# Dense projections cut by contraction steps over the slots of four mixers

## The reference

```python
for layer in range(DEPTH):                                   # DEPTH = 2
    need_ctx = layer < DEPTH - 1
    mod_l = adaln_params(c, w_mod[layer], b_mod[layer])      # silu(c) @ w_mod + b_mod, 6 parts of 1024
    mod_c = adaln_params(c_ctx, w_mod[layer], b_mod[layer])
    p_l = split_cols(modulate(x, norm1_g[layer], mod_l[0], mod_l[1]) @ w_in[layer])
    p_c = split_cols(modulate(ctx, norm1_g[layer], mod_c[0], mod_c[1]) @ w_in[layer])
    a_l, a_c = diff_attention(...)            # DA: softmax minus lambda times a second softmax
    b_l, b_c = hgrn2_mixer(...)               # HG: gated recurrence in both directions
    n_l, n_c = neighbourhood_attention(...)   # NA: 8 x 16 window on the 8 x 64 grid, and the context
    w_l, w_c = window_gqa(...)                # SW: band of 128 tokens, and the context
    x = x + mod_l[2] * (concat([a_l, b_l, n_l, w_l]) @ w_out[layer])
    x = x + mod_l[5] * (square(relu(modulate(x, norm2_g[layer], mod_l[3], mod_l[4]) @ w_ff1[layer])) @ w_ff2[layer])
    # with need_ctx the same for ctx with mod_c
```

## Time and profile before

| | us |
|---|---|
| median of 3 runs (2523.86 to 2529.58) | 2527.3 |
| profiled execution | 2523.21 |
| its span | 2521.4 |
| TensorE busy (82% of the span) | 2078.6 |
| VectorE busy (46%) | 1159.5 |
| ScalarE busy (30%) | 766.8 |
| GpSimd busy (24%) | 610.0 |
| mean granted clock | 0.908 |

### The profile page before, as it was taken

One profiled execution on the slowest core, in us unless ns is written; L12 is line 12 of the kernel. 1 busy time (PEld: TensorE's weight loads), 2 busy tenths in 40 slices (PEclk: granted clock), 3 DMA queues, 4 the chain that ended last, 5 costly groups with the idle time before them and its releaser, 6 DMA issues.

```text
span 2521.4 us, 29860 instructions
## 1 busy us (share of the span) xinstructions
PE 2078.6 (82%) x12484; PEld 1705.4 (68%) x12484; DVE 1159.5 (46%) x1782; ACT 766.8 (30%) x1225; POOL 610.0 (24%) x263
## 2 busy tenths in 40 slices
PE   5779786687775698999999997879688639899998
PEld 3667564466664586888888885658477536688887
DVE  2544536555499715222221316454685884522322
ACT  2522222223333325222221315232344432522321
POOL 0121010001166122222222221301001552344432
PEclk9889797778898798999999998989799778999999
DMA  7312020323165011122112212111001011232231
GB/s 261 59 51 84 1 67 1 101 88 80 42 204 193 5 51 49 52 67 67 57 62 67 68 50 39 55 33 34 17 18 51 0 34 51 67 100 88 96 100 67
DMA packets 178918, 168.86 MB, mean 67 GB/s; under 512 B 29200, under 2 KB 176096, under 8 KB 178656
## 3 DMA queue, kind: packets, MB, share of 16 engines
q1 hardware_dynamic: 176704, 161.18, 20.9%
q10 hardware_dynamic: 2080, 5.77, 0.8%
HBM read 159.07 MB, written 2.10 MB: 64 GB/s over the span
## 4 chain that ended last, share of the span: by engine, by line
PE 67%; DVE 17%; ACT 9%; issue 4%; POOL 2%; DMA 1%; ACTq 0%; SPq 0%; DVEq 0%; POOLq 0%
PE gp L691 53%; PE sp L823 3%; PE gp L858 2%; ACT DA_p L1184 2%; POOL HGx_kd L613 2%; PE sp L734 1%; PE tp L838 1%; ACT nt L1097 1%; PE sp L814 1%; PE gp L712 1%; DVE small L1578 1%; DVE sp L1453 1%; PE sp L921 1%; DVE sp L1452 1%; DMA raw<-in_w_mod 1%
## 5 line engine op out<-in xcount | busy, mean ns | idle before, releaser
L637 POOL TENSOR_TENSOR wlo<-raw,whi 128x2048 fp32r<-128x2048 f32 x98 | 452.4, 4617 | 1684.3 <-ACT whi L1079 1684.1
L691 PE MATMUL gp<-xhi,whi 128*128 128x512 f32 (+1 forms) x1584 | 584.1, 369 | 114.5 <-DVE xlo L1473 53.0
L691 PE MATMUL gp<-xlo,whi 128*128 128x512 f32 (+1 forms) x1584 | 570.8, 360 | 0.0
L691 PE MATMUL gp<-xhi,wlo 128*128 128x512 f32 (+1 forms) x1584 | 569.3, 359 | 0.0
L691 PEld LDWEIGHTS gp<-xhi,whi 128*128 128x128 f32 x1584 | 312.1, 197 | 170.2 <-issue 55.8
L691 PEld LDWEIGHTS gp<-xlo,whi 128*128 128x128 f32 x1584 | 311.7, 197 | 43.0 <-issue 1.7
L691 PEld LDWEIGHTS gp<-xhi,wlo 128*128 128x128 f32 x1584 | 310.8, 196 | 43.2
L1079 ACT ACTIVATE whi<-raw 128x2048 fp32r<-128x2048 f32 x98 | 186.8, 1908 | 426.3 <-PE gp L691 425.2
L1833 DVE SCALAR_TENSOR_TENSOR xT<-gp,mods,xT 128x512 f32<-128x512 f32 x120 | 78.6, 662 | 475.9 <-PE gp L691 475.9
L691 PE MATMUL gp<-hhi,whi 128*128 128x512 f32 (+1 forms) x768 | 273.7, 356 | 9.3 <-ACT frel L1393 6.3
L691 PE MATMUL gp<-hlo,whi 128*128 128x512 f32 (+1 forms) x768 | 272.1, 354 | 0.0
(11 more groups left out here) (304 smaller groups left out, 2864.3 us busy)
## 6 DMA issues: line engine op xcount, KB each, us to landing
raw<-in_w_ff SPq DMA_DIRECT2D x64, 1024.0 KB, 5.3
raw<-in_w_mod SPq DMA_DIRECT2D x48, 1024.0 KB, 5.3
raw<-in_w_in SPq DMA_DIRECT2D x20, 1024.0 KB, 5.1
raw<-in_w_in SPq DMA_DIRECT2D x24, 256.0 KB, 4.3
raw<-in_w_out SPq DMA_DIRECT2D x8, 768.0 KB, 4.7
bias<-e SPq DMA_DIRECT2D x96, 32.0 KB
xin<-in_x ACTq DMA_DIRECT2D x1, 2048.0 KB, 9.2
raw<-in_w_out SPq DMA_DIRECT2D x16, 128.0 KB, 4.7
```

The costliest lines, as they stand in the source:

```text
L637: nc.gpsimd.tensor_tensor(wlo[:, s % 2, :, :], raw[:, index[splits[s]] % 2, :, :], whi[:, s % 2, :, :].bitcast(F32), ALU.subtract).then_in ...
L691: mm = pe.matmul(out, lhs, rhs, start=(i == 0 and j == 0), stop=(i == KT - 1 and j == 2))
```

## The change

The table of filler is made anew. A dense group may now be cut along its contraction: a slot holds (unit, group, first step, end step), and a group that is begun in one slot goes on in the next in the same bank. Work is weighed and dealt out evenly over the slots of a mixer. All modulations leave NA and SW. Layer 0 has 14 in DA and 10 in HG (before: 4, 2, 12 and 22), layer 1 has 7 in DA and 9 in HG (before: none). Rows and turns of one modulation stand in neighbouring slots. The other engines walk a table ENDS with only the groups that end in a slot.

ScalarE rounds a weight unit as soon as the unit that used the same rounded buffer is done; only where the unit two places before is a modulation must its row have been reached.

VectorE reads all groups that end in a slot, except the last, before `finish`, and the last behind it.

```diff
-    mods = [("mod", 0, j, i) for j in range(2, 6) for i in range(4)] + [("mod", 1, j, i) for j in range(6) for i in range(4)]
+    mods = [("mod", l, j, i) for l, js in ((0, range(2, 6)), (1, range(6))) for j in js for i in range(4)]
+    counts = {("NA", 0): 0, ("SW", 0): 0, ("DA", 0): 14, ("HG", 0): 10, ("NA", 1): 0, ("SW", 1): 0, ("DA", 1): 7, ("HG", 1): 9}
...
+                k0 = 0
+                for k in range(KT):
+                    done += w
+                    if done * n >= (s + 1) * total and k < KT - 1:
+                        slots[s].append((u, c, k0, k + 1))
+                        k0 = k + 1
+                        s = min(s + 1, n - 1)
+                slots[s].append((u, c, k0, KT))
...
 FILL = fill_plan()
+ENDS = {key: [[(u, c) for u, c, _, b in slot if b == KT] for slot in slots] for key, slots in FILL.items()}
...
-            def dense(u, *cs, ready=None):
+            def dense(u, *cs, ready=None, part=range(KT)):
                 s = split_no[u] % 2
-                if cs[0] == chunks_of(u)[0]:
+                if cs[0] == chunks_of(u)[0] and part[0] == 0:
                     pe.wait_ge(lo_done, split_no[u] + 1)
                 for c in cs:
-                    start_group(N(u, c))
+                    if part[0] == 0:
+                        start_group(N(u, c))
...
             def after_unit(u):
 
-                reached[0] = max(reached[0], index[u])
+                reached[0] = max(reached[0], last_group(u))
                 while nexts[0] < len(splits):
                     s = nexts[0]
                     v = splits[s]
-                    if index[v] - 2 > reached[0]:
+                    before = units[index[v] - 2]
+                    if before[0] == "mod" and last_group(before) > reached[0]:
                         return
-                    before = units[index[v] - 2] if index[v] >= 2 else None
-                    if before and before[0] == "mod" and last_group(before) > last_group(u):
-                        return
-                    if s >= 2 and last_group(splits[s - 2]) > last_group(u):
+                    if s >= 2 and last_group(splits[s - 2]) > reached[0]:
                         return
...
                 if which == 1:
-                    wait_read(dve, ("mod", 0, 1, 3) if l == 0 else ("mod", DEPTH - 1, 5, 3))
+                    wait_read(dve, ("mod", l, 1, 3))
...
+                    fill(ENDS[m, l][n][:-1])
                     finish(n + 1)
-                    fill(FILL[m, l][n])
+                    fill(ENDS[m, l][n][-1:])
                     output(n)
```

More of the change, by code:

```diff
@@ L139, in fill_plan @@
         tiles = 6 if l < DEPTH - 1 else 4
-        for m, names, n_mods, n_slots in (("NA", ("SWq", "SWkv"), 4, 2 * tiles), ("SW", ("DAq", "DAk", "DAv"), 2, 2 * tiles),
-                                          ("DA", ("HGq", "HGi"), 12, 4 * tiles), ("HG", (), 22, 6 * tiles)):
-            items = [(("prj", l, n), c) for n in names for c in chunks_of(("prj", l, n))]
-            todo = [mods.pop(0) for _ in range(n_mods if l == 0 else 0)]
-            slots = [[] for _ in range(n_slots + 1)]
-            work = [[x] for x in items]
-            for i, u in enumerate(todo):
-                work.insert((i + 1) * (len(items) + i) // (len(todo) + 1) if items else i, [(u, "row"), (u, "turn")])
-            last = -1
-            for i, w in enumerate(work):
-                a = i * n_slots // len(work)
-                if len(w) == 2:
-                    slots[a].append(w[0])
-                    slots[a + 1].insert(0, w[1])
-                else:
-                    slots[a] += w
+        for m, names, n in (("NA", ("SWq", "SWkv"), 2 * tiles), ("SW", ("DAq", "DAk", "DAv"), 2 * tiles),
+                            ("DA", ("HGq", "HGi"), 4 * tiles), ("HG", (), 6 * tiles)):
+            chunks = [(("prj", l, name), c) for name in names for c in chunks_of(("prj", l, name))]
+            units = [mods.pop(0) for _ in range(counts[m, l])]
+            work = []
+            put = 0
+            for i, (u, c) in enumerate(chunks):
+                work.append((u, c, 2 if c[0] != "tok" and c[1] == 0 else 1))
+                closing = i + 1 < len(chunks) and chunks[i + 1][0] != u
+                while not closing and put < len(units) * (i + 1) // len(chunks):
+                    work.append((units[put], "row", 3))
+                    put += 1
+            work += [(u, "row", 3) for u in units[put:]]
+            total = sum(8 * w if c != "row" else 4 for _, c, w in work)
+            slots = [[] for _ in range(n + 1)]
+            s, done, turn = 0, 0, None
+            for u, c, w in work:
+                if c == "row":
+                    if turn:
+                        slots[s].append(turn)
+                    slots[s].append((u, "row", 0, KT))
+                    turn = (u, "turn", 0, KT)
+                    done += 4
+                    s = min(max(s + 1, done * n // total), n)
+                    continue
+                if turn:
+                    slots[s].append(turn)
+                    turn = None
+                k0 = 0
[6 more added lines that the diff above has]
+                slots[s].append((u, c, k0, KT))
+                if 10 * done * n >= (10 * s + 6) * total:
+                    s = min(s + 1, n - 1)
+            if turn:
+                slots[s].append(turn)
@@ L179, in dense_order @@
         for m in ("NA", "SW", "DA"):
-            groups.extend((u, c, one) for slot in FILL[m, l] for u, c in slot)
+            groups.extend((u, c, one) for slot in FILL[m, l] for u, c, a, _ in slot if a == 0)
         for n in ("HGf0", "HGf1", "HGg"):
             whole(("prj", l, n))
-        groups.extend((u, c, both) for slot in FILL["HG", l] for u, c in slot)
+        groups.extend((u, c, both) for slot in FILL["HG", l] for u, c, a, _ in slot if a == 0)
         for j in range(4):
@@ L721, in fill @@
             def fill(slot):
-                for u, c in slot:
+                for u, c, a, b in slot:
                     if u[0] == "mod":
@@ L725, in fill @@
                     else:
-                        dense(u, c)
+                        dense(u, c, part=range(a, b))
             def norm_sums(l, which, ks):
@@ L1283, in hgrn @@
                         if idx >= 4:
-                            fill(FILL["HG", l][idx - 4])
+                            fill(ENDS["HG", l][idx - 4])
                         idx += 1
                 read_out(ntile - 1)
-                for slot in FILL["HG", l][-5:]:
+                for slot in ENDS["HG", l][-5:]:
                     fill(slot)
```

23 lines of the change are left out of this document (12 added, 11 removed).

## The result

The changed kernel takes 2541.0 us (median of 5 runs, 2536.9 to 2543.3) against 2527.3 (also the median of 5 runs now): the ratio is 1.0050, with an interval of 1.0037 to 1.0064. It is slower by half a per cent, 13 us above the forecast of 2528. That is inside the whole range, 2505 to 2549, and outside the 2518 to 2538 that the forecast gave itself.

The account below looks back on a forecast made before the run. The prediction took TensorE's chain as the bound, with VectorE the floor in short DA slots and the bound in HG. Its terms summed to +0.5 us on 2523.2: 2523.7, or 2528 for the median; range 2505 to 2549.

Parts of the forecast that it names:

- HG: HG of both layers: 0.24 us per modulation; twelve fewer in layer 0 give -2.9, nine more in layer 1 +2.2.
- NA of layer 1: NA, layer 1: same work in equal pieces, two waits go and two handovers come; +1.5 us.
- DA of layer 0: DA, layer 0: slots of 147.8 us plus low clock sum to 161.4 against 178.1, -16.7; bounds -30 and +2.
- NA and SW of layer 0: NA and SW, layer 0: modulations, waits and low clock leave; -15.9 and -14.2 us.
- A slot of DA: Slots of DA: TensorE goes on 1.3 us after an early-read turn; 3.9 stays in slots 3, 5, 15, 17.
- DA of layer 1: DA, layer 1: seven modulations come with VectorE as floor; 117.7 against 89.0 us, +28.7; bounds +14 and +36.
- The end of DA: End of DA: late HGf0 and HGf1 loads hold the squares on ScalarE; +10.6 us in layer 0, +6.8 in layer 1.
- a sign of being wrong: Wrong if HG changed by more than 7, DA of layer 1 below 105, or squares within 2 us of last value product.
- rival 3: Low clock after each bank handover costs 1.2 instead of 0.4 in DA's 22 short gaps: +18, 2546 us; chance 0.25.
- Rival 2: The two stalls behind late loads, at the ends of DA, do not decide: -17.4, 2511 us; chance 0.11.
- rival 1: Modulations in DA of layer 1 are cheap, 1.55 us each: -14, DA of layer 0 -8; 2506 us; chance 0.20.
- The lock's price beside the sum: VectorE and GpSimd's shared port lock: remainders under softmax, three in SW, one in DA, some 4 us; sum would be +4.0.

Follow-up runs that it names:

- e7: The kernel before with only ScalarE rounding a weight unit as soon as its rounded buffer is free; 2520.4 us, ratio 0.9969.
- e6: The changed kernel with every read put ahead of the softmax whose bank is wanted again in the same slot; 2527.2 us, ratio 0.9993.
- e1: The changed kernel with all 16 modulations of layer 1 moved into HG of layer 0, which then has 26; 2508.0 us, ratio 0.9928.
- e5: The changed kernel with the modulations of DA put two chunks earlier in both layers; 2514.9 us, ratio 0.9940.
- e4: The changed kernel with the old modulation counts: 4, 2, 12 and 22 in layer 0, none in layer 1; 2507.5 us, ratio 0.9915.
- e12: The changed kernel with HG's rows spread evenly and each turn in the slot behind its row, both layers; 2536.1 us, ratio 1.0027.
- e2: The changed kernel with nine modulations moved from HG of layer 1 to HG of layer 0, which then has 19; 2535.8 us, ratio 1.0040.
- e9: The kernel before with early rounding on ScalarE and the first reads of a slot ahead of the softmax; 2483.4 us, ratio 0.9815.
- e8: The kernel before with only VectorE's reads of all groups of a slot but the last put before the softmax; 2486.5 us, ratio 0.9832.
- e10: e9 with the six modulations of NA and SW of layer 0 moved into HG (28 there), groups whole; 2467.1 us, ratio 0.9755.
- e3: The changed kernel with useless TensorE work in HG of layer 0: rows spread, turns over two slots and issued six times; 2547.1 us, ratio 1.0080.
- e11: Modulation places of e10, split table for DA of layer 0 alone, e6's read order, rows two chunks earlier; 2473.1 us, ratio 0.9788.

## Why the prediction came out as it did

The range held, and the sign of most terms; the forecast itself, no change, was 13 us too low. That it was no more is partly luck: by the traces HG came out 14.7 us above its terms and NA of layer 1 5.8, while DA of layer 0 came out 4.1 below. Taken by its steps:

- **NA and SW of layer 0: right.** -17.3 and -13.4 against -15.9 and -14.2. e7 shows the wait for `wlo` alone to be worth 6 to 8 us. Neither of the two profiled executions had the collision of the last section in NA; with it, the same instructions took 141, and NA's part would have been near -9.
- **A slot of DA: right.** 3.9 behind turns that are a slot's only end, 1.3 behind the others; e6 takes the first away for 13.4 us. From end of scores to end of scores the four slots with the long wait took 12.5, 12.4, 12.2 and 12.2 us, against 10.4 and 2.0 of low clock in the forecast. DA of layer 0 came to 157.3 against 161.4, DA of layer 1 to 116.9 against 117.7. The second total is right for a partly wrong reason: I gave the split one piece's late read and the modulations 3.6 each, and e1 gives the split 12 and each modulation 2.2.
- **The end of DA: right**, +13.7 and +6.4 against +10.6 and +6.8, and e5 shows the loads to be the cause. The squares came 12.8 us behind the value product where I had 11.4.
- **HG: the step that failed.** I priced a modulation at 0.24 us in either layer, from the difference of the two layers per level, took twelve away for -2.9 and added nine for +2.2. Over the same cut as the forecast's, layer 0 went up by 8.6 us and layer 1 by 9.4, both more than the 7 that I had named as a sign of being wrong (6.7 and 7.3 in the levels of the table). In layer 0 the number of modulations has no price that the runs show: 19, 22 and 26 took 105.9, 104.8 and 106.7 in the new placing, and 10 took 104.0 to 108.1. What shows is the place of the turn. With 22 modulations the new placing cost 3.4 us more than the old (e4 against before), with 10 it cost 2.5 to 6.6 more (e5 and the changed kernel against e12). The old placing gave 101.4 to 101.6 in all five kernels that have it with 10 or 22; with 28, where loads are waited for, it took 104.2 and 108.6. The difference between "turn in the next slot" and "turn with the next row" stood in the code, and I did not price it. In layer 1 it is the price that was too low: the new kernels without modulations there took 61.3 us (e1, e2, e4), so nine cost 6.6 to 9.7, 0.7 to 1.1 each, above my upper 0.58. No run shows why these three are 2.4 below the kernel before, or why one table of layer 0 takes 104.0 in one execution and 108.1 in another.
- **NA of layer 1: half of it.** Forecast +1.5, traced +7.3. The unchanged program took 122.4 in e7 to e9 against 118.1 in the profile shown, and the changed one 120.9 to 125.8; so some 3 us of it are the change's (TensorE waits 2.1 us where the second tile of SWq ends in the middle of a slot), and some 4 are which execution was profiled. No run shows what makes those 4; it isn't the collision that layer 0 has.
- **Rivals.** None of the three came true. The low clock after each short handover (rival 3, 2546) gives nearly the time measured, but by a mechanism that isn't there: DA of layer 0 is below the forecast, where it had it 18 above. Rival 2 is excluded by e5, rival 1 by DA of layer 1. The lock's price beside the sum, +4.0, didn't come either: in SW of layer 0 one softmax operation took 0.97 instead of 0.48 under a remainder, in DA of layer 0 one took 3.33 instead of 0.35 and in SW of layer 1 one 4.87 instead of 0.55, but the two stretches of SW came out within 0.8 us of the forecast.

The largest thing that I didn't see was no cost but a gain: read order alone is worth 43 us in the old table (e8), more than all I had for DA. In the changed kernel it was spent again by the seven modulations and the cuts in layer 1 (28 us), the two ends of DA (20) and the modulations and placing in HG (14 in the traces).

The form of the old table was the better one for the new order of reads. From e10 to the changed kernel there are 74 us. e5's move gave 26 and e1's 33, and they overlap at the end of DA in layer 1; they were not run together.

## What to carry to other kernels

Order the reads of a shared bank on the consuming engine by when the bank is wanted again; look for that before dealing out work more evenly, since a cut that ends alone in a slot creates a new late read. Before a movable load is placed late, ask what its buffer's next load is for and which engine has it in strict order ahead of the work that everyone waits for. A price per item taken from the difference of two stages can hide a price of position: compare the tables of both kernels in each stage, those that "only lose work" too.

## What the runs showed of the hardware

NA of layer 0 comes in two lengths, 133 and 141 us for the same instructions, by a collision of VectorE and GpSimd. In the seven executions with the new table and no modulations in NA, one `NA_lo` subtraction took 5.2 us in those that needed 141 (e1, e3, e5, e12) and none did in those that needed 133 (e2, e6, and the changed kernel itself). One is as long in e4, e9 and e11, and none in the kernel before, e7, e8 and e10. VectorE's three `NA_lo` subtractions, and what GpSimd did beside them, first in the changed kernel, then in e12:

```profile
135.77 3.87 DVE L1557 TENSOR_TENSOR NA_lo<-NA_xr,NA_hi 128x768 fp32r<-128x768 f32 x3
```

```profile
128.74 11.38 POOL L677 TENSOR_TENSOR bias<-bias,cf 128x256 f32<-128x256 f32 x12 [19.10 <-DMA bias<-e]
140.08 4.55 POOL L663 TENSOR_TENSOR wlo<-raw,whi 128x2048 fp32r<-128x2048 f32 x1
```

```profile
135.28 7.74 DVE L1563 TENSOR_TENSOR NA_lo<-NA_xr,NA_hi 128x768 fp32r<-128x768 f32 x3
```

```profile
127.06 9.97 POOL L683 TENSOR_TENSOR bias<-bias,cf 128x256 f32<-128x256 f32 x12 [18.11 <-DMA bias<-e]
137.00 5.20 POOL L669 TENSOR_TENSOR wlo<-raw,whi 128x2048 fp32r<-128x2048 f32 x1
```

In e12 the tables of the bias land 1.7 us earlier and VectorE's first of the three starts 0.5 earlier; GpSimd is done with the tables at 137.0 instead of 140.1, its long subtraction starts inside VectorE's stretch, and the three take 7.74 us instead of 3.87. TensorE waits for what follows, 12.3 instead of 8.3:

```profile
140.68 0.80 PE L719 MATMUL gp<-xhi,whi 128*128 128x512 f32 x1 [8.28 <-DVE NA_vt L1578]
```

```profile
144.05 0.80 PE L725 MATMUL gp<-xhi,whi 128*128 128x512 f32 x1 [12.33 <-DVE NA_vt L1584]
```

and in the stretch behind it its clock falls once more: the granted clock is 0.50 from 160 to 165 us and 0.84 from 165 to 180 in e12, and 1.00 from 150 us on in the changed kernel. So 4 us become 8. Here the slower stage is the one whose transfer landed earlier. The Trainium skill, "SBUF — State Buffer", on SBUF's two separate sides, says that whichever of the two engines starts first holds the shared port pair for its whole instruction; the added 3.9 us, a little under one GpSimd subtraction (4.6 undisturbed), agree. Of VectorE's four `NA_lo` subtractions in e12 one took 5.24 us and the others 1.3 (duration in ns, shortest, median, longest):

```profile
L1563 DVE TENSOR_TENSOR NA_lo<-NA_xr,NA_hi x4: 1268/1326/5243, 129.7 to 137.8; 128x768 fp32r<-128x768 f32 x4
```

In e3 TensorE's records add up to 99 of 108 us, and its mean granted clock was 0.82; in e12, with the rows in the same slots and every turn issued once, they add up to 72 of 101.5 us, and it was 0.89. I had expected the reverse. Why is not settled: no run varied the added work by itself.
